# Moving a quarter's coefficients and mix ahead of the next group's routing piece on VectorE

## What is computed

```python
def peer(y, w_q, sub_keys, u, v):
    q = (yt @ w_q).reshape(T, PEER_HEADS, 2, PEER_HALF)
    s = jnp.einsum('thpc,pnc->thpn', q, sub_keys)
    val, idx = lax.top_k(s, PEER_TOPK)
    cand = val[:, :, 0, :, None] + val[:, :, 1, None, :]
    top_val, top_pos = lax.top_k(cand..., PEER_TOPK)
    expert = ...                      # 16 of 16384 experts for each token and head
    gate = jax.nn.softmax(top_val, axis=-1)
    act = gate * gelu(einsum('thkd,td->thk', u[expert], x))
    return einsum('thk,thkd->td', act, v[expert])
```

## Time and profile before

| | |
|---|---|
| median of 3 runs | 1707.58 us (1706.82 to 1708.81) |
| the profiled execution, its own time | 1707.35 us |
| its span, first to last instruction | 1705.6 us |
| TensorE matmuls busy | 1081.4 us (63%) |
| VectorE busy | 1096.2 us (64%) |
| ScalarE busy | 425.7 us (25%) |
| GpSimd busy | 506.5 us (30%) |
| HBM read over the span | 622.31 MB, 365 GB/s |
| gathers | 528, 14.7 us from issue to landing in the median |
| mean granted TensorE clock | 0.749 of full speed |

### The profile page before, as it was taken

One profiled execution on the slowest core, in us unless ns is written; L12 is line 12 of the kernel. 1 busy time (PEld: TensorE's weight loads), 2 busy tenths in 40 slices (PEclk: granted clock), 3 DMA queues, 4 the chain that ended last, 5 costly groups with the idle time before them and its releaser, 6 DMA issues.

```text
span 1705.6 us, 18928 instructions
## 1 busy us (share of the span) xinstructions
PE 1081.4 (63%) x6580; PEld 716.0 (42%) x6580; DVE 1096.2 (64%) x3024; ACT 425.7 (25%) x881; POOL 506.5 (30%) x554
## 2 busy tenths in 40 slices
PE   6999984434444457786765458776768455554455
PEld 5887971111111126664544227665556222222222
DVE  1123257777777776797665675787766777777773
ACT  1401011111111114773210113773312221211110
POOL 0000033333333331333332331333322333433330
PEclk9999995566655569887898569888879765656655
DMA  4324479999999999999999999999999999999995
GB/s 143 116 87 144 189 306 406 421 413 419 410 413 420 413 416 417 379 394 392 385 418 418 417 415 418 388 374 381 365 419 414 419 412 414 422 418 410 410 416 217
DMA packets 97103, 624.61 MB, mean 366 GB/s; under 512 B 10608, under 2 KB 12656, under 8 KB 29424
## 3 DMA queue, kind: packets, MB, share of 16 engines
q0 software_dynamic: 76032, 553.68, 79.0%
q1 hardware_dynamic: 18528, 68.23, 10.8%
q10 hardware_dynamic: 2448, 1.49, 0.3%
HBM read 622.31 MB, written 1.05 MB: 365 GB/s over the span
## 4 chain that ended last, share of the span: by engine, by line
DMA 38%; PE 27%; DVE 16%; POOL 7%; issue 5%; ACT 5%; DVEq 2%; ACTq 0%; POOLq 0%; SPq 0%
DMA ring<-in_uv_dram,expert 32%; PE ps L531 11%; DVE ring L942 7%; POOL ring L330 7%; DMA wring<-in_wall_dram 6%; PE ps L687 4%; ACT diag L433 2%; PE ps L700 2%; PE ps L642 2%; DVE cv L992 2%; PE ps L645 2%; PE ps L538 1%; PE ps L675 1%; PE ps L567 1%; DVE picked L934 1%
## 5 line engine op out<-in xcount | busy, mean ns | idle before, releaser
L942 DVE CUSTOM_DVE_ANT_0 ring<-ring,ps 128x1024 f32<-128x1024 f32 x528 | 634.0, 1217 | 305.9 <-DMA ring<-in_uv_dram,expert 225.8
L330 POOL DMA_INDIRECT ring<-in_uv_dram,expert x528 | 498.7, 944 | 1032.9 <-DVE expert L936 473.3
L687 PE MATMUL ps<-ring,mix 128*32 128x512 f32 x2112 | 383.2, 863 | 399.2 <-DVE mix L958 399.2
L687 PEld LDWEIGHTS ps<-ring,mix 128*32 128x32 f32 x2112 | 69.6, 140 | 606.4 <-DVE mix L958 459.7
L531 PE MATMUL ps<-yT,wring 128*128 128x128 f32 (+2 forms) x1392 | 229.7, 327 | 48.8 <-DMA wring<-in_wall_dram 33.0
L531 PEld LDWEIGHTS ps<-yT,wring 128*128 128x128 f32 x1392 | 204.0, 205 | 79.6 <-DMA wring<-in_wall_dram 37.6
L506 ACT ACTIVATE gel<-dots 128x4 f32<-128x4 f32 x132 | 27.1, 205 | 821.3 <-DVE dots L942 820.9
L700 PE MATMUL ps<-sel,osb 128*128 128x16 f32 x528 | 86.0, 308 | 77.5 <-ACT osb L492 77.5
L700 PEld LDWEIGHTS ps<-sel,osb 128*128 128x128 f32 x528 | 82.6, 246 | 112.4 <-ACT osb L492 112.4
L433 ACT ACTIVATE diag<-ident,params 128x128 f32<-128x128 f32 x310 | 96.5, 389 | 16.9 <-PE ps L729 15.8
L729 PE MATMUL ps<-gz,diag 128*128 128x128 f32 x620 | 84.8, 299 | 2.4 <-ACT diag L433 1.2
(11 more groups left out here) (147 smaller groups left out, 1130.3 us busy)
## 6 DMA issues: line engine op xcount, KB each, us to landing
wring<-in_wall_dram SPq DMA_DIRECT2D x112, 512.0 KB, 9.8
ring<-in_uv_dram,expert POOLq DMA_INDIRECT x528, 14.7
ring<-in_wall_dram SPq DMA_DIRECT2D x4, 2048.0 KB, 16.6
hT<-in_xT_dram SPq DMA_DIRECT2D x2, 544.0 KB, 5.3
out_dram<-fo ACTq DMA_DIRECT2D x16, 64.0 KB, 7.3
params<-in_smalls_dram ACTq DMA_DIRECT2D x1, 430.0 KB, 5.0
```

The source lines that it names most:

```text
L330: pool.indirect_dma_start(out=ring[:, i % R, :], out_offset=None, in_=uv, in_offset=bass.IndirectOffsetOnAxis(ap=expert[:, n % 2, k:k + 1] ...
L687: mm = pe.matmul(po[32 * j:32 * j + 32, half, :], mix[:, k, :], ring[:, slot, D + 512 * half:D + 512 * (half + 1)], start=(q == 0), stop=( ...
L942: nc.vector.tensor_tensor_reduce(out=row, in0=row, in1=yrep, scale=1.0, scalar=0.0, op0=ALU.mult, op1=ALU.add, accum_out=dots[:, k:k + 1]) ...
```

## The change

In VectorE's list, `weights(n, q)` stands ahead of the routing piece of the next group. Nothing else differs: the same instructions, waits, buffers and semaphores, in another order on one engine.

```diff
@@ -1072,6 +1072,7 @@
                             side(n, q - 1, i)
                         elif n:
                             side(n - 1, 3, i)
+                    weights(n, q)
                     if n + 1 < N:
                         if q == 0:
                             route_best(n + 1)
@@ -1079,7 +1080,6 @@
                             route_pairs(n + 1)
                         if q == 2:
                             route_experts(n + 1)
-                    weights(n, q)
                     if q == 0 and n:
                         add_back(n - 1)
                     if q == 0 and n > G0 + 1:
```

## The result

The changed kernel takes 1728.1 us in the median of 4 runs (1726.12 to 1733.87), the kernel before 1708.19 us (1706.82 to 1709.01). The ratio is 1.0123, 95% interval 1.0097 to 1.0149: 1.2% slower, 20 us. Forecast were 1716.7 us and a range of 1709 to 1728. One run of one later kernel took 1949.76 us at a lower clock and is left out of that kernel's numbers.

A forecast was written before the change was run, and what follows sets the result against it. The prediction took the 16 DMA engines as the bound, so only late gathers into a dry queue cost time. Terms 3.6 + 2.6 + 1.4 + 1.5 + 0 = 9.1 us on 1707.35 gave 1716.5, forecast 1716.7 us, range 1709 to 1728.

The forecast's parts named there:

- the earlier mix: Mix comes a piece earlier, 2.2 to 3.7 us, as do `values` and ring slots; counted 0, down to -8 us.
- Does 0.6 us hurt?: Ordinary groups, quarter 2: expert numbers come 0.6 us later, hidden by queued gathers; counted 0, at most 12 us.
- The margin of 1.5 us: Ordinary groups' end: 4.6 us of queue left, a new gather needs 3.1 to begin; margin falls from 1.5 to 0.9.
- My own sign for this rival: DMA share in 345 to 425 us, ordinary groups: stays at 1.01 if the forecast holds, falls if the first rival does.
- The first rival: Ordinary groups lose too, as gathers begin later on loaded engines: 6 to 12 us more, about 1726 us; chance 0.18.
- Convolution, quarters 0 and 1: Groups 11 to 13 and 19 to 21: VectorE waits uncovered for late Gelus; with quarter 2's 0.4 each, 3.6 and 2.6 us.
- the 5.5 by which group 24's numbers were to be late: Group 23's third piece must wait for a late Gelu, numbers coming at 1318.4; counted 1.4 us (0 to 2.3).
- Group 0: The routing pieces wait for the Gelu: 1.3 us in quarter 0, 0.6 in quarters 1 and 2; 1.5 of 1.9 counted.
- the 9.1 of the sum: Whole loss forecast: convolutions 3.6 and 2.6, group 23 1.4, group 0 1.5, and 0 for mix coming earlier.
- The faster rival: Groups 12 to 14 and 20 to 22: earlier mix issues gathers 2 us sooner; gain at most 8 us, 1703.5 us; chance 0.11.
- The second rival: Convolution: ScalarE's and TensorE's chain sets the pace and swallows VectorE's 6.2 us; under 3 us left, 1708 to 1711; chance 0.16.

The follow-up runs named there:

- 0.50 and 0.83 us of delay: Kernel before plus one or two idle VectorE comparisons ahead of `route_experts` in the 20 ordinary groups; ratios 1.0010 and 1.0077 to the kernel before.
- quarter 2 alone: Against the kernel before, `weights` ahead of the routing piece only in quarter 2 of each group; ratio 1.0070, 12.1 us slower.
- early pieces: Kernel before with `route_best` and `route_pairs` in quarter 0, `route_experts` in quarter 1: ratio 0.9907 with `weights` behind them, 0.9968 with `weights` ahead.
- quarters 0 and 1 alone: Against the kernel before, `weights` ahead of the routing piece only in quarters 0 and 1 of each group; ratio 1.0041, 7.1 us slower.

## Why the prediction was right or wrong

**The bound and the direction** were right: the DMA engines set the pace, the end of `route_experts` is what counts in the ordinary groups, and the earlier mix brought nothing that a trace shows.

**The step that failed** is "Does 0.6 us hurt?" in the ordinary groups, put at 0 with a bound of 12 us. Three things in it were off.
- The delay was 0.8 us, not 0.6. The two instructions and the drain behind them take 0.61 us, where I had 0.43. The runs with 0.50 and 0.83 us of delay lie on either side of where the loss begins.
- The margin of 1.5 us took the 16 DMA engines for one queue. It counted four whole gathers of 2.5 us still to move; but the bytes fell to 307 GB/s between 1398 and 1400 us, when by that count 2 to 4 us of queue were left. A gather lands when the last of the engines is done, and most of them are done earlier: in the first trace, 14 of 16 engines' signals for group 9's first gather came within 5.15 to 5.71 us of its issue, the last two after 6.23 and 7.00. The engines that are ahead run dry first, which is free; 0.8 us later the last ones do too, and that is the loss. How late varies from group to group, from 0 to 1.4 us over the first two gathers, and why is open.
- The evidence, "a share of 1.01 shows no dip", was an average over two groups that could not show one. My own sign for this rival, that share falling below 1.01, came as 1.00, too coarse to read without the bytes.

The runs put this term, which I had at 0, at 13 us (the 0.8 us delay alone), 12 (quarter 2 alone, with what it does in the busy groups) and 9 to 13 by the milestones and landings of the first pair of traces. In the trace of the changed kernel from the later chip it is about 5, by the last dots. The first rival had the place and its price of 6 to 12 us right, at a chance of 0.18; its time of 1726 us was 2 us from the result. That a gather begins later on loaded engines, which it gave as the reason, is not shown.

**The Trainium skill's rule** (DMA: Bandwidth & Descriptors, latency and other measured facts), that a DMA's fixed cost grows under HBM load, pointed to the right side. But no run here shows that cost. The shortest times from issue to landing, 5.6 us, belong to gathers before which the queue is nearly or quite empty, and the unevenness of the engines explains the dip of the kernel before without it. For the loss after the change the rule and the uneven queue were not told apart.

**Convolution, quarters 0 and 1.** The exchange of the waits was right: in group 11 `add_back` no longer waited. Between the expert numbers of groups 10 and 15, 3.6 us were forecast and 2.1 measured. Between those of 18 and 24, 2.6 plus the 5.5 by which group 24's numbers were to be late, 8.1 in all, were forecast; 9.3 were measured. Group 0 had 1.9 and measured 2.6. Outside the ordinary groups the first comparison lost 10.7 us in all, against the 9.1 of the sum. The run with the move in these groups alone gives 5.0 us (1.9 to 8.1) for the same 9.1, but net of the stop that it avoids, and with early pieces, where neither of the two kernels has a stop of that size, the same move costs 10.4. So this part of the sum was right to within a few us; that it stands on single traces is its weakness.

**The faster rival** (the wait of gathers for `values` is ended by mix) fell. Mix stood 3.5 us earlier in group 25, quarter 2, and the ordinary stretches moved fewer bytes; groups 10 to 14 took 2.1 us more and groups 18 to 23 took 9.3 more.

**The second rival** (the waits hide in each other) fell with quarters 0 and 1 alone at 7.1 us (3.3 to 10.7), where it left under 3.

## What to carry to other kernels

When one resource is full all the time, ask how many microseconds of work stand in its queue at the moment when the next batch is put in, and look at that moment in stretches of 2 us: a busy share over a whole period hides a dip of 1%. Then ask whether the dip costs time: engines that finish first may rest for free while the last of them set the pace, and only a further slip reaches those. An instruction order that lets the producer of the next batch slip by less than a microsecond can cost nearly that much in every period, while tens of microseconds of idle time on an engine beside it cost little. Here the better move was the other one: find the next batch's indices a quarter earlier, after which the same slip costs nothing. Its gain of 0.9% came mostly from the convolution groups, where those indices had been late.

## What the runs showed that was not expected

- The busy share of the 16 DMA engines reads 1.01 both at 415 and at 421 GB/s, and more bytes per second need not mean shorter groups: at 421 GB/s a group was 0.1 us shorter.
- The 16 landing signals of one indirect gather come about 2 us apart, so a queue that is 4.6 us long for the last of them leaves the first ones dry. With a queue that never runs dry they drift apart to 6 us within eight groups.
- The kernel before differs by 12 to 15 us between the first comparison and all later ones (1708 against 1720 to 1724 us), while the changed kernel stays at 1728 to 1729. One cause seen is a stop of 6.6 us on TensorE, seen only in kernels that keep the old order in quarter 2 there; why it occurs is open. On one chip its runs spread from 1716.17 to 1730.05 us, so the 0.2% that can be told apart hold for the first comparison only.
